# Moving weight rings, arena and coefficients by 192 and 256 bytes in SBUF

## What is computed

```python
# first block
h = modulate(rmsnorm(x, norm_mix), shift_m, scale_m)          # shift, scale, gate = silu(c) @ w_ada + b_ada
proj = h @ w_in                                               # 1024 x (512 + 1024 + 1536 + 16)
x = x + gate_m * (concat([pool_mixer(...), ssd_mixer(...)]) @ w_out)
h = modulate(rmsnorm(x, norm_ffn), shift_f, scale_f)
x = rmsnorm(x + gate_f * peer(h, w_query, keys, expert_down, expert_up), norm_final)
# second block
p = rmsnorm(x, norm1) @ w_in_2                                # 1024 x 7168: gated recurrence and convolution
x = x + merged @ w_out_2
x = rmsnorm(x + peer_2(rmsnorm(x, norm2), ...), final_g)
# peer: per token and head, the best 16 of 128 x 128 experts by two key lists;
#   out = sum over experts of gate * gelu(h . down[e]) * up[e],  16384 experts of 1024 numbers
```

## The kernel before, in words

| tile | bytes | address | modulo 512 |
|---|---|---|---|
| xT, h_hi, h_lo | 8192 each | 1152, 9344, 17536 | 128 |
| prm | 1080 | 25728 | 128 |
| cst | 2048 | 26816 | 192 |
| ring, ring_hi, ring_lo | 12288 each | 28864, 41152, 53440 | 192 |
| arena | 131072 | 65728 | 192 |
| wf, w_hi, w_lo | 4096 each | 196800, 200896, 204992 | 192 |
| xs_lo | 8192 | 214464 | 448 |

## Time and profile before

### The profile page before, as it was taken

One profiled execution on the slowest core, in us unless ns is written; L12 is line 12 of the kernel. 1 busy time (PEld: TensorE's weight loads), 2 busy tenths in 40 slices (PEclk: granted clock), 3 DMA queues, 4 the chain that ended last, 5 costly groups with the idle time before them and its releaser, 6 DMA issues.

```text
span 2035.6 us, 37757 instructions
## 1 busy us (share of the span) xinstructions
PE 1988.1 (98%) x14131; PEld 1843.6 (91%) x14131; DVE 1508.9 (74%) x2593; ACT 1013.5 (50%) x1358; POOL 0.2 (0%) x4
## 2 busy tenths in 40 slices
PE   7999999999999999999999999999999999999998
PEld 6988999999999888888799999999999998888886
DVE  5767768887886666666679666688878866666666
ACT  3641454455555444444546554444555554444444
POOL 0000000000000000000000000000000000000000
PEclk9999999999999999999999999999999999999999
DMA  7655767776556777778655655777766667787786
GB/s 272 197 202 188 279 198 241 232 233 207 183 181 212 241 241 241 242 239 242 204 165 156 188 158 158 232 234 232 233 206 186 187 219 237 241 241 240 241 243 190
DMA packets 135164, 440.82 MB, mean 217 GB/s; under 512 B 14992, under 2 KB 15248, under 8 KB 131472
## 3 DMA queue, kind: packets, MB, share of 16 engines
q1 hardware_dynamic: 117200, 406.84, 64.5%
q10 hardware_dynamic: 17856, 32.51, 4.4%
HBM read 403.64 MB, written 35.65 MB: 216 GB/s over the span
## 4 chain that ended last, share of the span: by engine, by line
PE 90%; DVE 5%; DMA 3%; ACT 1%; issue 1%; SPq 0%; DVEq 0%; ACTq 0%
PE ps L561 27%; PE ps L563 27%; PE ps L562 27%; PE ps L855 3%; DVE ring_lo L374 2%; PE ps L598 1%; DMA arena<-in_w_ada 1%; DMA ring<-in_down 1%; PE ps L704 1%; PE ps L831 1%; ACT ring_hi L368 1%; PE ps L554 0%; DVE arena L1855 0%; PE ps L784 0%; PE ps L955 0%
## 5 line engine op out<-in xcount | busy, mean ns | idle before, releaser
L374 DVE TENSOR_TENSOR ring_lo<-ring,ring_hi 128x1024 fp32r<-128x1024 f32 x632 | 772.9, 1224 | 311.1 <-ACT ring_hi L368 308.4
L368 ACT ACTIVATE ring_hi<-ring 128x1024 fp32r<-128x1024 f32 x632 | 667.7, 1057 | 634.4 <-PE ps L563 509.0
L561 PE MATMUL ps<-h_hi,ring_lo 128*128 128x256 f32 x2816 | 803.8, 285 | 20.0 <-DVE ring_lo L374 9.5
L562 PE MATMUL ps<-h_lo,ring_hi 128*128 128x256 f32 x2816 | 791.5, 281 | 0.0
L563 PE MATMUL ps<-h_hi,ring_hi 128*128 128x256 f32 x2816 | 791.4, 281 | 0.0
L561 PEld LDWEIGHTS ps<-h_hi,ring_lo 128*128 128x128 f32 x2816 | 534.4, 190 | 25.1 <-issue 20.6
L563 PEld LDWEIGHTS ps<-h_hi,ring_hi 128*128 128x128 f32 x2816 | 536.5, 191 | 0.0
L562 PEld LDWEIGHTS ps<-h_lo,ring_hi 128*128 128x128 f32 x2816 | 534.3, 190 | 0.4 <-issue 0.2
L561 PE MATMUL ps<-ring_hi,w_lo 128*128 128x512 f32 x1024 | 398.4, 389 | 0.0
L562 PE MATMUL ps<-ring_lo,w_hi 128*128 128x512 f32 x1024 | 398.3, 389 | 0.0
L563 PE MATMUL ps<-ring_hi,w_hi 128*128 128x512 f32 x1024 | 398.3, 389 | 0.0
(11 more groups left out here) (284 smaller groups left out, 1289.2 us busy)
## 6 DMA issues: line engine op xcount, KB each, us to landing
ring<-in_down SPq DMA_DIRECT2D x256, 512.0 KB, 4.3
ring<-in_up SPq DMA_DIRECT2D x256, 512.0 KB, 4.1
ring<-in_w_in SPq DMA_DIRECT2D x80, 512.0 KB, 3.7
kept_z<-wf ACTq DMA_DIRECT2D x124, 256.0 KB, 3.2
xT<-kept_z SPq DMA_DIRECT2D x124, 256.0 KB, 4.3
arena<-in_w_ada SPq DMA_DIRECT2D x24, 1024.0 KB, 9.7
ring<-in_wq SPq DMA_DIRECT2D x32, 512.0 KB, 4.1
ring<-in_w_out_ssd SPq DMA_DIRECT2D x8, 512.0 KB, 3.8
```

Of the source, the lines that this page charges most:

```text
L368: nc.scalar.activation(ring_hi[:, part_slot(m), :], ring[:, slot(m), :], ACT.Copy).then_inc(S("high"), 1)
L374: ns.tensor_tensor(ring_lo[:, part_slot(n), :], ring[:, slot(n), :], ring_hi[:, part_slot(n), :].bitcast(fp32), ALU.subtract)\
L561: mm(psum, s_lo, m_hi, start=start, stop=False)
L562: mm(psum, s_hi, m_lo, start=False, stop=False)
```

## The change

The parameter tile is declared 48 columns (192 bytes) longer, and `prm` is a view of its first 270 columns. An unused tile of 64 columns (256 bytes) is declared ahead of the arena. No instruction is added, removed or reordered.

```diff
-        prm = sb("prm", [P, NCOL])
+        prm_room = sb("prm_room", [P, NCOL + 48])
+        prm = prm_room[:, 0:NCOL]
         cst = sb("cst", [P, NCONST])
         ring = sb("ring", [P, RING, BLK])
         ring_hi = sb("ring_hi", [P, RING, BLK], fp32r)
         ring_lo = sb("ring_lo", [P, RING, BLK], fp32r)
+        sb("between", [P, 64])
         arena = sb("arena", [P, 32768])
```

## The result

The changed kernel takes 2053.41 us (median of 4 runs, 2053.06 to 2055.68), the kernel before beside it 2028.76 us (2025.22 to 2031.01): a ratio of 1.0131, 95% interval 1.0094 to 1.0167. It is slower by 1.3%, not faster by 2.5% as forecast. The profiled execution took 2055.68 us, its span 2053.9 us against 2035.6.

The account below looks back on a forecast made before the run. PE was taken as the bound, through the start-to-start distance of its matmuls. Savings of 29.5 us (h) and 20.5 us (`up`) made -50 us, a median of 1979 us; own range 1962 to 1990, with rival A 1962 to 2056 us.

Parts of the forecast that it names:

- What bounds the kernel: Whole kernel: time is the number of matmuls times their start-to-start distance; PE works 1988.1 of 2035.6 us.
- other engines' addresses don't matter: DVE and ACT work, such as the 128x1024 split: hardly feels the moved addresses, put at 0.
- 0 for the scaled stage: 576 matmuls with scaled activations: distances 256 and 0 merely swap, so 0 saved, at best 3.9 us.
- The h term: Matmuls with h moving: 6600 go from 117.8 to 113.3 ns at distance 256, 29.5 us saved.
- The up term: 3072 matmuls of 512 columns in `up`: 226.7 to 220.0 ns, 20.5 us saved.
- Rival A: All h matmuls: 256 is as bad as 0, h at 120.0, `up` unchanged, +25, 2054 us; chance 0.24.
- The difference is not part of the change: Profiled execution 2037.35 us against timed runs at 2029.05: this gap was taken as unaffected by the change.
- Rival B: The two uses part: h goes to 120.0 (+24.7), `up` gains 20 to 33 us, 2020 to 2033 us; chance 0.10.
- Rival C: All matmuls: loss lies in a larger period or the instruction form, rhythms stay, 2029 us; chance 0.13.
- Rival D: Top-16 stretches: DVE becomes the bound, half of 14 us lost, 1986 us; counted within the forecast's 0.40.

Follow-up runs that it names:

- f1: Kernel before with activations and coefficients each begun 16 bytes into longer tiles (h at 48, up at 16 modulo 512): 2067.90 us.
- f3: Kernel before with activations and coefficients each begun one element into longer tiles (h at 60, up at 4 modulo 512): 2090.66 us.
- e3: Kernel before with rings 64 bytes further, arena and coefficients 64 more (h at 128, up at 64 modulo 512): 2068.42 us.
- e12: Kernel before with 256 unused bytes ahead of cst alone (h at 320, up at 0): 2025.1 us, 1.0003 times before.

## Why the prediction was wrong, point by point

**What bounds the kernel** was right: PE's rate, start to start, was what moved the time, and the counts of the earlier trace rows gave its size. That other engines' addresses don't matter was right too (the split of DVE takes 1224 ns before, after and in f1, 1223 in f3), as was 0 for the scaled stage.

**The h term** was the step that failed. It took the loss at 256 as 6.7 ns, "the nearest row of this kind of matmul". The row nearest in distance was another: the earlier trace rows has `xs_lo` at exactly 256 from the ring, at 120.0. I set it aside as no pure case. It was true: 256 costs 13.3 ns, and the 1500 matmuls at 113.3 and the 6600 at 117.8 all went to 120.0. Behind it stood a picture, that farther apart is better, which two points (0 and 64) can't carry when the effect is periodic: 64 and 192 are alike, and so are 0 and 256. (The product 6600 x 4.5 ns is 29.7 us, not 29.5; that changes nothing.)

**The up term** failed as well: 220.0 was carried over from h to a stream of another length, and 256 gave 226.7 like 0. The loss being 13.3 ns for both at distance 0 had been read as one loss per load for either kind. At 64 they part: 6.7 or 11.1 ns for h, 20.0 for `up` (e3). Of the twelve other distances tried, 256 was as good as 0 and none was better, so `up` had nothing to gain from any of them.

**Rival A** named the mechanism with its place and size: 256 as bad as 0, h at 120.0, `up` unchanged, 2054 us; measured 2053.41. Its reason that a period shorter than 512 may rule was the right one of its two. It had 0.24, because I counted the only direct row for less than a general picture. Part of the agreement is chance. Its +24.7 us was for the profiled execution, where h rose by 18.7 us. Within the streams (distances under 140 ns) h did rise by 24.8 us; but the longer distances, those with a break, fell from 60.5 to 54.4 us, and PE's idle time before the first of the three lines from 20.0 us to 16.2. Slower matmuls seem to have had less to wait for. In the medians it is +24.6 us, because the timed runs of before lie 8.6 us below its profile, those of after 2.3 us below. **"The difference is not part of the change"** was wrong too, as far as the spreads tell: the profiled execution of before had 117.8 ns in nearly all of both top-16 stretches, a slow draw, and after the change there is no draw left.

**Rival B** had h right and `up` wrong. **Rival C**, no change, fell with h at 120.0. **Rival D** was never reached. The rule of the Trainium skill ("TensorE: Matmul & The Clock Gate", section "Wait — 56ns, not 53.3ns?"), a gap of N / 2.4 + 2.5 ns, would have had no change. It failed as a statement on these matmuls in 18 kernels: none had 109.2 or 215.8 ns, and 256-column ones went from 113.3 to 122.2 by addresses alone. The Trainium skill's page "SBUF — State Buffer", section "Who interferes with whom", has PE waiting for nobody. These runs don't show it waiting for another engine either, but PE's pace does depend on how far apart its own two operands lie.

## What to carry to other kernels

Where PE is the bound, count matmuls per stretch and compare the distance with the columns; if some ns are missing, look at the distance in bytes between stationary and moving operand before anything else, and move it by single steps, since the effect repeats (here h at 64, 192, 320 and 448) and differs between kinds of matmul: what is best for `up` is bad for h. If the trace has one row at the very distance that a change will set, that row is worth more than a trend through two others. And when executions of one kernel spread by a per cent while those of its variant don't, a rhythm may be drawn anew in each; compare the medians of many executions, not two profiles.

## What was not expected of the hardware

- For 256-column fp32r matmuls with a load each, the distance from start to start depends on how far apart the two operands lie: 113.3 or 117.8 ns at 64, 192, 320 and 448 bytes modulo 512, 120.0 at 0 and 256, 118.7 or 120.0 at 128; at 60, one element beside 64, it is 122.2.
- For 512-column ones, which have the ring as the moving operand, it is 226.7 ns at 0 and 256 modulo 512, 228.3 to 228.9 at 448 and 496, and 232 to 233.4 at 4, 16, 32, 64, 128, 192, 384, 480 and 504.
- At 64 modulo 128 a stream without breaks keeps one of two rhythms for 200 us (1725 matmuls), and the next stream of the same execution may keep the other (e12: 113.3, then 117.8).
